# Layers of a first block in token halves around their norms, with the second norm carried into the next stage

## The reference

```
h = layer_norm(DN_ALPHA * h + mix, ln1_g[layer], ln1_b[layer])
ffn = conv_ffn(h, f_w_in[layer], f_conv_w[layer], f_conv_b[layer], f_w_out[layer])
h = layer_norm(DN_ALPHA * h + ffn, ln2_g[layer], ln2_b[layer])
```

## Time and profile before

| | us |
|---|---|
| median of 3 runs (lowest, highest) | 3899.38 (3898.45, 3903.36) |
| the profiled execution | 3904.11 |
| its span in the profile | 3902.3 |
| granted TensorE clock, mean | 0.965 |

### The profile page before, as it was taken

The page is one execution under the profiler, slowest core; times in us unless marked ns, Lnnn a source line. Parts: engine busy times, 40 slices in busy tenths (PEclk is TensorE's granted clock), DMA queues, the critical chain, the costliest instruction groups (busy, mean ns, idle before and its releaser), DMA issues. The chain is left out here.

```text
span 3902.3 us, 61579 instructions
## 1 busy us (share of the span) xinstructions
PE 3639.2 (93%) x26368; PEld 3149.9 (81%) x26368; DVE 2055.4 (53%) x3337; ACT 1385.0 (35%) x2155; POOL 86.0 (2%) x143
## 2 busy tenths in 40 slices
PE   8989999699889997999997889999999997889998
PEld 8989999588789996888875668888888875658886
DVE  6747653444476635443358665444443358665443
ACT  5624332455443323222233343223222233343221
POOL 0000000011000000000000000000000000000000
PEclk9999999899899998999998999999999997999999
DMA  4222232122122331333310013333333310013332
GB/s 141 70 87 77 92 93 82 56 72 77 50 76 87 94 91 66 97 94 98 103 53 2 17 65 98 97 96 99 97 96 94 106 54 2 18 55 97 98 92 76
DMA packets 86847, 303.73 MB, mean 78 GB/s; under 512 B 9632, under 2 KB 9760, under 8 KB 86320
## 3 DMA queue, kind: packets, MB, share of 16 engines
q1 hardware_dynamic: 86576, 299.80, 24.6%
HBM read 297.63 MB, written 2.13 MB: 77 GB/s over the span
## 5 line engine op out<-in xcount | busy, mean ns | idle before, releaser
L605 DVE TENSOR_TENSOR two_w_lo<-two_raw,two_w_hi 128x1024 fp32r<-128x1024 f32 (+1 forms) x338 | 405.4, 1200 | 803.2 <-ACT two_w_hi L596 800.3
L620 PE MATMUL psum<-two_x_hi,two_w_hi 128*128 128x512 f32 x1808 | 707.0, 391 | 27.5 <-DVE two_w_lo L605 27.5
L620 PE MATMUL psum<-two_x_lo,two_w_hi 128*128 128x512 f32 x1808 | 704.4, 390 | 0.0
L620 PE MATMUL psum<-two_x_hi,two_w_lo 128*128 128x512 f32 x1808 | 704.4, 390 | 0.0
L596 ACT CAST two_w_hi<-two_raw 128x1024 fp32r<-128x1024 f32 (+1 forms) x338 | 346.3, 1026 | 842.2 <-PE psum L620 838.5
L1550 PE MATMUL psum<-one_x_hi,one_w_hi 128*128 128x264 f32 x1408 | 401.2, 285 | 23.1 <-DVE one_x_lo L1694 21.1
L620 PEld LDWEIGHTS psum<-two_x_hi,two_w_hi 128*128 128x128 f32 x1808 | 340.0, 188 | 99.9 <-DVE two_w_lo L605 28.3
L1550 PE MATMUL psum<-one_x_lo,one_w_hi 128*128 128x264 f32 x1408 | 400.2, 284 | 0.0
L1550 PE MATMUL psum<-one_x_hi,one_w_lo 128*128 128x264 f32 x1408 | 399.9, 284 | 0.0
L620 PEld LDWEIGHTS psum<-two_x_lo,two_w_hi 128*128 128x128 f32 x1808 | 339.9, 188 | 72.3 <-issue 1.4
L620 PEld LDWEIGHTS psum<-two_x_hi,two_w_lo 128*128 128x128 f32 x1808 | 339.9, 188 | 70.8
(11 more groups left out here) (429 smaller groups left out, 6490.4 us busy)
## 6 DMA issues: line engine op xcount, KB each, us to landing
two_raw<-in_swi_in SPq DMA_DIRECT2D x172, 512.0 KB, 3.6
one_raw<-in_ffn_in SPq DMA_DIRECT2D x88, 512.0 KB, 3.6
two_raw<-in_swi_out SPq DMA_DIRECT2D x64, 448.0 KB, 3.3
two_raw<-in_mix_in SPq DMA_DIRECT2D x54, 512.0 KB, 3.6
one_raw<-in_attn_w SPq DMA_DIRECT2D x32, 512.0 KB, 3.8
two_raw<-in_swi_out SPq DMA_DIRECT2D x32, 512.0 KB, 3.5
one_raw<-in_ffn_out SPq DMA_DIRECT2D x32, 448.0 KB, 3.4
one_raw<-in_lru_w SPq DMA_DIRECT2D x24, 512.0 KB, 3.6
```

The source lines that it names most:

```text
L605: self.nc.vector.tensor_tensor(self.m.ws.lo[:, u % self.SLOTS, w], self.m.raw[:, u % self.RAW, w], self.m.ws.hi[:, u % self.SLOTS, w].bitc ...
L620: last = self.nc.tensor.matmul(self.m.ps[:, bank, :], a[:, u % self.SLOTS, w], b[:, k0 + k, :], start=(start and k == 0 and q == 0), stop= ...
```

## The change

In `layer_stage` the last APART output tiles (3 in layer 0 and 4 in layer 1 ahead of ln1, 1 ahead of ln2) are multiplied for token half 0 and then for half 1, their units kept or in slots; half 0 is emptied, summed and normalised while half 1 is multiplied. All instructions of the norms are 264 wide (a class `LayerNorm`). The first four units behind ln1 (three and a fourth that has a place of its own) are multiplied for half 0 tile by tile, then three of them for half 1, then the fourth. For ln2, half 1 of the last tile is left in PSUM, and the class `Carried` takes it up in the next stage: VectorE's `take` (scale, add), `add`, `add_square`, then `moments`, `invert` and `scale`/`rest` for both halves, between the splits of the first units. The next stage's unit 0 (`early`) and the forget weights are loaded and split in the layer's stage. Attention's first eight chunks have banks of their own and run in two passes, the forget sums beside them; chunks 8 and 9 come ahead of the steps, and steps 2 and 3 have one chunk each. `chain_stage` does the same with its units 0 to 3; the masks are loaded at its start and their stage is gone. SP's order in the attention behind `c_ready` stays.

```diff
-def load_masks_stage(nc, m, d):
-    with stage(nc, "load_masks", "loaded") as (block, s):
-        @block.sync
-        def _(sp):
-            sp.dma_start(m.masks[:, :], d["masks"]).then_inc(s["loaded"], 16)
-            sp.wait_ge(s["loaded"], 16)
...
+        self.homes = homes or {}
+        self.ring = [u for u in range(len(units)) if u not in self.homes]
+        self.turn = {u: n for n, u in enumerate(self.ring)}
...
+    def freed(self, u):
+        if u in self.homes:
+            return self.homes[u][2]
+        n = self.turn[u] - self.SLOTS
+        return self.ring[n] + 1 if n >= 0 else 0
...
+            def halves(rms):
+                def piece(u, h, k):
+                    (hi, lo), w = st.place(u), slice(k * P, (k + 1) * P)
+                    for q, (a, b) in enumerate(((hi, m.xs.hi), (hi, m.xs.lo), (lo, m.xs.hi))):
+                        ins = nc.tensor.matmul(m.ps[:, u, rms.half[h]], a[:, w], b[:, k, rms.half[h]],
+                                               start=(k == 0 and q == 0), stop=(k == KT - 1 and q == 2))
+                    return ins
+                for k in range(KT):
+                    pe.wait_ge(s["x_lo"], k + 1)
+                    piece(0, 0, k)
+                    if k == 1:
+                        ln.sums(pe, 1, 1)
+                for u in range(1, 4):
+                    pe.wait_ge(s["w_lo"], u + 1)
+                    if u == 3:
+                        pe.wait_ge(ln.s["out_ready"], 1)
+                    for k in range(KT):
+                        piece(u, 0, k)
+                for k in range(KT):
+                    pe.wait_ge(s["x_lo"], KT + k + 1)
+                    for u in range(4):
+                        ins = piece(u, 1, k)
+                        if k == KT - 1:
+                            ins.then_inc(s["unit_done"], 1)
+                st.multiply(pe, 4, 4, m.xs, 0, True, True)
+                rms.total(pe)
+                st.multiply(pe, 5, 5, m.xs, 0, True, True)
...
+                tile(0, 0)
+                ln.square(act)
+                st.split_hi(act, 2)
+                tile(0, 1)
+                tile(0, 2)
+                ln.square_of_mean(act, 1)
+                st.split_hi(act, 3)
+                tile(0, 3)
+                ln.root(act, 1)
+                tile(0, 4)
+                st.split_hi(act, 4)
+                for k in range(5, KT):
+                    tile(0, k)
+                st.split_hi(act, 5)
+                for k in range(KT):
+                    tile(1, k)
+                for k in range(KT):
+                    norm[0].square(act, k)
+                    if k == 4:
+                        st.split_hi(act, 6)
+                st.split_hi(act, 7)
...
+    FIRST = [(q, h) for h in range(2) for q in range(4)]
+    BANKS = (0, 1, 2, 4, 3, 5, 1, 0)
...
+            return ((10, 11), (12, 13), (14,), (15,))[i]
...
-            sp.dma_start(at.forget_raw[:, :], d["forget_w"]).then_inc(s_["forget_loaded"], 16)
             for n in range(4):
                 sp.sem_inc(s_[f"loaded{n}"], 16)
             sp.wait_ge(s_["c_ready"], 1)
...
+            def first_pair():
                 for k in range(KT):
+                    pe.wait_ge(ln.s["x_lo"], k + 1)
+                    forget(0, k)
+                    piece(0, 0, k, BANKS[0])
+                    if k == 1:
+                        ln.sums(pe, 1, 1)
+                for q in range(1, 4):
+                    pe.wait_ge(s_["w_lo"], q)
+                    for k in range(KT):
+                        piece(q, 0, k, BANKS[q])
+                pe.wait_ge(s_["chunk_out"], 2)
+                for k in range(KT):
+                    pe.wait_ge(ln.s["x_lo"], KT + k + 1)
+                    last = forget(1, k)
+                    if k == KT - 1:
+                        last.then_inc(s_["forget_psum"], 1)
+                    for q in range(4):
+                        piece(q, 1, k, BANKS[4 + q])
...
-            forget()
+            first_pair()
             pe.wait_ge(s_["soft_own"], 1)
             pe.wait_ge(s_["low_own"], 1)
-            for n in range(8):
-                chunk(n)
             turn_values(0)
             score(0)
+            chunk(8)
+            chunk(9)
...
+            ln.affine(act, 0, 0)
+            ln.square(act)
             split_hi(1)
+            ln.affine(act, 0, 1)
+            ln.affine(act, 0, 2)
+            ln.square_of_mean(act, 1)
+            split_hi(2)
+            ln.affine(act, 0, 3)
+            ln.root(act, 1)
+            ln.affine(act, 0, 4)
+            split_hi(3)
+            for k in range(5, KT):
+                ln.affine(act, 0, k)
+            empty(0)
+            for k in range(KT):
+                ln.affine(act, 1, k)
+                if k in (2, 4, 6):
+                    empty(k // 2)
...
+            for n in range(4, 8):
                 empty(n)
-                if n % 2 and n // 2 + 2 <= 4:
-                    split_hi(n // 2 + 2)
+            split_hi(4)
+            split_hi(5)
             open_gate(0)
             keep_values(0)
+            empty(8)
+            empty(9)
...
+    APART = (KEPT_TILES[l], 1)
+    first_apart = [KT - n for n in APART]
+    apart = [range(first_apart[p], KT) for p in range(2)]
+    base = (0, KT + APART[0])
+    done = lambda p, t, h=0: base[p] + (t if t < first_apart[p] else first_apart[p] + h * APART[p] + t - first_apart[p]) + 1
+    last = lambda p, h: done(p, KT - 1, h)
+    half = lambda p, t: p * APART[0] + t - first_apart[p] + 1
+    between = ({1: 6, 4: 7}, {0: 5, 1: 6, 3: 7})[l]
+    ahead = (((4, 5), (6, 7), (8, 9), (11, 13), (15, 16)), ((3, 4), (5, 6), (7, 8), (9, 10)))[l]
+    ahead_apart = ((17, 18, 19), (11, 12, 12, 12))[l]
+    EXTRA = OU + 3
     pads = [[m.pads[:, 2 * j + g, 0:T1 + 2] for g in range(2)] for j in range(2)]
...
+        homes = {OU - G * APART[0] + n: (m.kept.hi[:, n, :], m.kept.lo[:, n, :], 0) for n in range(G * APART[0])}
+        homes[EXTRA] = (m.kept_gate.hi, m.kept_gate.lo, OU - G * (APART[0] - 1) if l == 0 else 0)
+        st = Stream(nc, m, s, units, homes)
+        norm = [LayerNorm(nc, m, s, f"ln{p + 1}", l, p == 0 or l == 0, 2 * p, 2 * KT * p, 2 * KT * p) for p in range(2)]
...
+                for t in apart[p]:
+                    to = bank(t, 0)
+                    for n, (a, b) in enumerate(parts):
+                        ins = multiply(u + len(parts) * t + n, to, src, a, n == 0, n == len(parts) - 1, (0,))
+                    ins.then_inc(s["half_done"], 1)
+                for t in apart[p]:
+                    to = bank(t, 1)
+                    for n, (a, b) in enumerate(parts):
+                        multiply(u + len(parts) * t + n, to, src, a, n == 0, n == len(parts) - 1, (1,)).then_inc(
+                            s["unit_done"], 1)
+                        if t == first_apart[p] and n == 0:
+                            norm[p].sums(pe, 0, last(p, 0))
 
             output(0, 0, hidden, spans)
...
+            for h in range(2):
+                for k in range(KT):
+                    pe.wait_ge(s["x_lo"], KT * h + k + 1)
+                    for u in range(4 - h):
+                        if h == 0 and k == 0:
+                            pe.wait_ge(s["w_lo"], OU + u + 1)
+                        ins = product(OU + u, h, 2 * u, m.xs, 0, k, k == 0, k == KT - 1)
+                        if h == 1 and k == KT - 1:
+                            ins.then_inc(s["unit_done"], 1)
+                    if h == 0 and k == 2:
+                        norm[0].sums(pe, 1, last(0, 1))
+            multiply(OU + 3, 6, m.xs, 0, True, True, (1,)).then_inc(s["unit_done"], 1)
...
+            for n, t in enumerate(apart[0]):
+                square(0, t, 0)
+                st.split_hi(act, ahead_apart[n])
+            norm[0].square_of_mean(act, 0)
+            norm[0].root(act, 0)
+            square(0, first_apart[0], 1)
+            st.split_hi(act, OU + 4)
             for k in range(KT):
-                affine(0, "ln1", k, True)
+                norm[0].affine(act, 0, k)
+                if k in between:
+                    square(0, between[k], 1)
+                if k == KT - 3:
+                    norm[0].square_of_mean(act, 1)
+            norm[0].root(act, 1)
+            for k in range(KT):
+                norm[0].affine(act, 1, k)
             for t in range(FT):
                 j, u = t % 2, OU + 2 * t
-                st.split_hi(act, u + 4)
+                st.split_hi(act, u + (4 if t else 6))
...
+            norm[1].moments(dve, 0)
+            norm[1].invert(dve, 0)
+            norm[1].scale(dve, 0, 0)
 
...
-    chain_stage(nc, m, d, "chain0", [("ffn", 0, 1), ("mix_in", 0, 0)])
+    chain_stage(nc, m, d, "chain0", [("ffn", 0, 1), ("mix_in", 0, 0)], True)
```

More of the change, by code:

```diff
@@ L744, in first_units @@
             def first_units(part, rms, banks):
-                ready = (s["x_lo"], KT * part.p)
+                ready = (s["x_lo"], rms.split)
                 if part.first:
@@ L765, in _ @@
```

(41 more changed lines are left out.)

572 lines of the change are left out of this document (369 added, 203 removed).

## The result

The changed kernel takes 3874.6 us (median of 4 runs, 3869.7 to 3878.2) against 3900.8 us before on the same chip; the ratio is 0.993 with a 95% interval from 0.9918 to 0.9941. The forecast was 3864 us, in a range of 3845 to 3880, and faster with a chance of 0.91. The profiled run took 3872.5 us, its span 3870.6.

A forecast was written before the change was run, and what follows sets the result against it. TensorE is 93% busy, so only its idle time at four layer-norm junctions counts, bound there by VectorE's norm instructions. Gains of 10.2 + 9.9 + 2.6 + 12.8 = 35.5 us off 3899.4 give 3864 us, range 3845 to 3880.

The forecast's parts named there:

- rival C: Norm steps at all four junctions: half-width instructions cost three quarters of whole ones, 1.5 us a tile; 3876 us, 22%.
- signs: Profile marks of a right forecast, among them TensorE's wait on `one_x_lo` falling from 10.5 to single waits under 2 us.
- J1: Junction at layer 0's ln1: 16.5 us lost before, 6.3 after, a gain of 10.2 us.
- J3: Junction at layer 1's ln1: 16.5 us lost before, 6.6 after, a gain of 9.9 us.
- J2: Junction at layer 0's end and the attention's start: 38.8 us lost before, 36.2 after, a gain of 2.6 us.
- J4: Junction at layer 1's end and `chain0`: 32.5 us lost before, 19.3 plus 0.4 after, a gain of 12.8 us.
- Half-width instructions: Norm steps on VectorE and ScalarE: 1.25 us a tile, reciprocal 1.75 us, ScalarE's passes 0.61 us each.
- The two waits: Attention's start, behind late forget sums: TensorE waits 4.3 us before the values' turn and 12.0 us for unit 4's weights.
- norm and banks alone would bring 19: Attention's start: without the new wait on the forget sums, norm and chunk banks would gain 19 us.
- Rival B: Attention's start: the c chain is covered after all, the 12.0 us wait and its 1.4 of clock go; 3851 us, 14%.
- The two waits behind it: `chain0`, behind its passes: 1.0 us for the late root mean square and 0.4 us for unit 7's split.
- Rival D: Passes over the tiles: TensorE's clock stays at half, each matmul costs 0.1 us more; slower, 3925 us, 4%.

The follow-up runs named there:

- banks: Changed kernel with the wait for the last FFN tile's evictions moved ahead of norm 2's first sums, only 21 awaited before the output tiles: 3873.7 us, one run.
- all: Changed kernel with loads first, forget first and banks, plus ScalarE's splits of units 4 and 5 between its chunk evictions: 3851.9 us, ratio 0.9867.
- loads first: Changed kernel with SyncE issuing the attention's loads of units 4 to 7 ahead of its wait for c_ready: 3867.5 us, ratio 0.9915.
- after: The changed kernel itself, against the kernel before: 3874.6 us, ratio 0.993.
- forget first: Changed kernel with forget sums and unit 0's half first in the first pair's second pass, units 1 to 3 following: 3873.4 us, ratio 0.9928.
- both: Changed kernel with the edits of loads first and forget first together: 3859.8 us, ratio 0.9893.
- gate between: Changed kernel with half 0 of the fourth FFN unit moved between the two passes in both layers: 3871.5 us, one run.
- keep two: Changed kernel with two instead of four of layer 1's output tiles having their second halves put off: 3887.4 us, one run.

## Why the prediction was right, and where it was short

**Direction and range: right.** 35.5 us were forecast in the junctions, 27.1 came; 3874.6 lies in the range, 10.6 above the number. By the number alone it is nearer to rival C's 3876, but C's mechanism didn't come, as the next step shows. One of the signs was too strict: single waits on `x_lo` under 2 us were forecast, and the longest are 2.3 in J1 and J3, 2.7 in J2 and 2.9 in J4. Step by step:

**Half-width instructions: right.** 1.25 us a tile forecast, 1.28 measured; the reciprocal 1.80 against 1.75, ScalarE's passes 0.61 as taken. Rival C (1.5) is out. The Trainium skill (VectorE: DVE Perf Modes, "The TRN2 errata — SBUF-src ops pay a fixed extra latency per instruction") has (N + 151) / 0.96 ns for an fp32 `tensor_tensor` addition. Worked out from it, an estimate for 264 columns is 432 ns, and the rows have 0.42 and 0.43. That is the duration alone, and what counts in this chain is the distance from start to start, 0.35 to 0.46.

**J1: 7.8 instead of 10.2.** From half 0's end to the first `x_lo` it is 12.2 us (forecast 11.6), to the last 39.0 (37.4). Counted from layer 0's first matmul, tile 2 starts 9.5 us sooner, where 11.0 was forecast (16.5 less 5.0 and 0.5). Behind it 0.3 is lost instead of 0.8, and then 1.4 at the wait on `one_pads`, which the forecast didn't have. So of the missing 2.4 some 1.5 is the norm's chain, mis-sized, and 1.4 the wait, less 0.5. The sum had a slip besides: 41.4 - 36.8 is 4.6 and not "about 5.0", so its own figures give a gain of 10.6.

**The step that failed: the wait for the last evictions.** The forecast has no term for the start of the FFN's output tiles; it took them to begin as before. They don't: all 22 of `emptied` are waited for ahead of the first output tile, where before it was 21, with the 22nd only ahead of the sums. In the whole diff these are two lines that look like tidying. The wait costs 1.35 us in J1 and in J3, 2.7 of the 8.4 missing, and 0.1 more in a slow matmul behind each; the run on the banks shows both go.

**J3: 7.0 instead of 9.9.** 1.35 is that wait. The rest is a term mis-sized: intervals over 0.121 us from the put-off halves up to and with the FFN's third tile sum to 8.1 us (0.121 taken off each), forecast 6.6. Waits of 0.92, 0.90 and 2.34 are in it, and the sums, which take 0.44 + 0.25 + 0.32 from start to start where 0.5 was taken.

**J2: right, for the reason given.** The two waits were forecast at 4.3 and 12.0 and are 4.1 and 11.6. The claim that norm and banks alone would bring 19 comes near: with both chains out of the way J2 gains 1.7 + 15.4 = 17.1. Rival B (3851, the chain covered by itself) was wrong for this kernel. That "all" comes to 3851.9 is chance: it removes other waits as well, and the run in which only the loads' wait goes, "loads first", is at 3867.5.

**J4: 10.5 instead of 12.8.** The stage's change took 1.34 us from the last matmul to VectorE's first step (1.0), the first pass 18.8 (18.3), half clock some 2 us of its matmuls (1.5), the sums 0.65 more in layer 1's last tile. The two waits behind it came nearly as forecast, 0.86 and 0.27 for 1.0 and 0.4. That makes some 1.7 of the missing 2.3; the rest is not assigned. The masks' stage was sized right, 3.5 by the run that puts it back.

**Rival D was half there.** J2's and J4's first passes were granted 0.59 and 0.54: fed a half tile at a time with waits up to 2.9 us, TensorE ran at 1.2 GHz for most of them (J2's had the full clock for some 3 us in its middle). That cost little inside them, since VectorE is slower still: in "all" the clock of J2's pass came back before its end, and the last `x_lo` ended at the same 16.4 us. The first 20 us of that pass in "all", as a window:

```profile
675.76:695.76 20.00, 13.86 (x75) 10.89 (x76) 16.57 (x34) 13.90 (x24) 0.00 (x0) 0.74 0.32 102
```

Behind the passes the slow clock cost some 1.3 and 1.6 us in the next 72 matmuls. The second passes, J1 and J3 have little or nothing of it. The Trainium skill (TensorE: Matmul & The Clock Gate, "A second HAM failure mode: psum-queue depth-cycling") tells of a clock that swings between its two levels when TensorE idles briefly between groups of matmuls. J2's first pass agrees, with 0.50, 1.00 and 0.50 again; J4's had 0.50 after its first 2 us; J3's passes kept the full clock, and J1's lost it once, behind the wait of 2.3.

## What to carry to other kernels

When work is moved so that it finishes later, walk every queue that waits for it, SP's too: a queue of loads behind one late semaphore, and the sums that this semaphore waits for, took back 15 of 17 us in J2 here, and moving the two brought them. Count each `wait_ge` whose number or place changes in the diff as a part of its own, however small. And where two elementwise engines pace a pass, take other work out of the pass first: here that gave 1.8 and 3.8 us in the two stretches, while TensorE's clock inside the pass made next to no difference.

## What was not expected of the hardware

The clock's return differs between runs of the same instructions. In J2, 20 to 24 us after its first pass began, the same 4 us were granted 0.93 (after), 0.96 (loads first), 0.86 (forget first), 0.86 (both), 0.73 (banks) and 1.00 (all; there already 1.00 at 16 to 20, where the others had 0.50). How much of a measurement's scatter comes from it is not shown. Behind `chain0`'s first hidden product the same code took from 2134.8 us (gate between, whole span granted 0.967) to 2146.1 (keep two, 0.963), which fits; but one run of the changed kernel was granted 0.931 in the mean and took only 3878.2. The last 200 matmuls of the attention, in short groups with waits between them, took 39.8 us after and 41.9 with both. TensorE's windows there, after and with both:

```profile
1014.40:1024.40 10.00, 7.78 (x45) 4.82 (x43) 2.95 (x11) 2.59 (x8) 0.00 (x0) 0.50 0.01 2
1024.40:1034.40 10.00, 4.31 (x33) 3.18 (x31) 2.62 (x5) 4.46 (x7) 0.00 (x0) 0.67 0.00 1
```

```profile
997.40:1007.40 10.00, 6.68 (x36) 4.39 (x38) 3.78 (x14) 3.63 (x14) 0.00 (x0) 0.50 0.01 2
1007.40:1019.40 12.00, 6.30 (x43) 4.20 (x39) 2.58 (x5) 4.42 (x7) 0.00 (x0) 0.50 0.00 1
```

The window at 20 to 24 us, "banks" first, then "all" (length, busy (count) PE, clock, DMA, GB/s):

```profile
695.03:699.03 4.00, 4.00 (x26) 0.73 0.00 0
```

```profile
695.76:699.76 4.00, 4.00 (x36) 1.00 0.00 0
```

What decides when it comes back was not tried.
